# The inverse of the gated delta rule: at two of its three levels, X is copied from a transpose of its own transpose, in place of a third product

## The reference

```python
kk = jnp.einsum('bhnid,bhnjd->bhnij', k, k)
m = jnp.where(strict, beta[..., :, None] * kk * decay, 0.0)
rhs = jnp.concatenate([v * beta[..., None], k * (beta * jnp.exp(g))[..., None]], axis=-1)
sol = lax.linalg.triangular_solve(m, rhs, left_side=True, lower=True, unit_diagonal=True)
...
v_new = u_c - jnp.einsum('bhcd,bhde->bhce', w_c, state)
```

## Time and profile before

| what | value |
|---|---|
| median of 3 runs | 1093.03 us (1093.01 to 1093.15) |
| profiled execution, its own time | 1092.93 us |
| span of that execution, first to last instruction | 1091.6 us |
| granted TensorE clock, mean | 0.999 |
| PE busy | 1079.7 us (99%) |
| DVE busy | 542.6 us (50%) |
| ACT busy | 562.0 us (51%) |
| POOL busy | 436.7 us (40%) |
| L643, PE and PEld records | 64 and 64, 8 of each per head and level |
| L2028 and L2037 | 8 instructions each |

### The profile page before, as it was taken

One profiled execution on the slowest core, in us unless ns is written; L12 is line 12 of the kernel. 1 busy time (PEld: TensorE's weight loads), 2 busy tenths in 40 slices (PEclk: granted clock), 3 DMA queues, 4 the chain that ended last, 5 costly groups with the idle time before them and its releaser, 6 DMA issues.

```text
span 1091.6 us, 14798 instructions
## 1 busy us (share of the span) xinstructions
PE 1079.7 (99%) x5661; PEld 885.1 (81%) x5661; DVE 542.6 (50%) x1135; ACT 562.0 (51%) x1042; POOL 436.7 (40%) x236
## 2 busy tenths in 40 slices
PE   8999999999999999999999999999999999999998
PEld 7877878788888888898778787789888888888886
DVE  3739789698765224152445455535111115544444
ACT  6546767767777642353556566554222224333333
POOL 4334342352532444552242332345444446444441
PEclk9999999999999999999999999999999999999999
DMA  9133121221312232722222321232333334332212
GB/s 258 50 96 88 48 70 48 68 68 47 86 53 78 78 97 97 245 70 75 79 77 69 87 78 59 78 94 79 99 97 97 97 97 134 98 98 97 97 56 77
DMA packets 140528, 97.23 MB, mean 89 GB/s; under 512 B 9013, under 2 KB 125090, under 8 KB 140458
## 3 DMA queue, kind: packets, MB, share of 16 engines
q1 hardware_dynamic: 138728, 95.03, 29.7%
q10 hardware_dynamic: 1730, 1.25, 0.4%
HBM read 94.14 MB, written 2.91 MB: 89 GB/s over the span
## 4 chain that ended last, share of the span: by engine, by line
PE 85%; DVE 10%; issue 2%; ACT 2%; DMA 1%; SPq 0%; POOL 0%; DVEq 0%; ACTq 0%
PE bank L481 24%; PE bank L1194 14%; PE bank L1212 14%; PE bank L522 5%; PE bank L891 4%; PE bank L865 4%; PE bank L875 4%; PE bank L1225 2%; DVE s L2089 1%; DVE g L1896 1%; DVE bank L2011 1%; DVE multipliers L2009 1%; PE bank L496 1%; PE bank L1040 1%; PE bank L1002 1%
## 5 line engine op out<-in xcount | busy, mean ns | idle before, releaser
L2472 POOL TENSOR_TENSOR ring<-raw_ring,ring 128x1024 fp32r<-128x1024 f32 x160 | 389.4, 2437 | 566.8 <-ACT ring L1239 566.8
L481 PE MATMUL bank<-hT,ring 128*128 128x512 f32 x1536 | 392.0, 402 | 0.5 <-ACT rawsb L1314 0.5
L481 PEld LDWEIGHTS bank<-hT,ring 128*128 128x128 f32 x1536 | 278.5, 188 | 58.7 <-issue 6.5
L1239 ACT CAST ring<-raw_ring 128x1024 fp32r<-128x1024 f32 x160 | 167.3, 1047 | 109.5 <-PE bank L1212 88.8
L1194 PE MATMUL bank<-hT,ring 128*128 128x512 f32 x672 | 152.5, 389 | 0.0
L1212 PE MATMUL bank<-ring,ring_u 128*128 128x512 f32 x672 | 152.5, 389 | 0.0
L1212 PEld LDWEIGHTS bank<-ring,ring_u 128*128 128x128 f32 x672 | 126.1, 188 | 26.2
L1194 PEld LDWEIGHTS bank<-hT,ring 128*128 128x128 f32 x672 | 126.1, 188 | 26.1
L2447 DVE TENSOR_TENSOR ring_u<-u,ring_u 128x1024 fp32r<-128x1024 f32 x32 | 80.7, 2529 | 73.8 <-ACT ring_u L1811 73.8
L2452 DVE TENSOR_TENSOR u<-u 128x512 f32<-128x512 f32 x32 | 22.9, 715 | 138.8 <-ACT u L1818 138.8
L1818 ACT ACTIVATE u<-bank 128x512 f32<-128x512 f32 x32 | 19.1, 598 | 114.8 <-PE bank L1194 108.3
(11 more groups left out here) (293 smaller groups left out, 1474.4 us busy)
## 6 DMA issues: line engine op xcount, KB each, us to landing
raw_ring<-in_w_in SPq DMA_DIRECT2D x144, 256.0 KB, 3.3
raw_ring<-in_w_up SPq DMA_DIRECT2D x64, 256.0 KB, 3.2
raw_ring<-in_w_down SPq DMA_DIRECT2D x64, 256.0 KB, 2.8
raw_ring<-in_w_out SPq DMA_DIRECT2D x32, 256.0 KB, 2.9
x<-in_x SPq DMA_DIRECT2D x8, 512.0 KB, 5.0
raw_ring<-in_w_branch_sb SPq DMA_DIRECT2D x8, 256.0 KB, 2.8
raw_ring<-in_w_branch_gdn SPq DMA_DIRECT2D x8, 256.0 KB, 3.3
cum<-cums SPq DMA_DIRECT2D x4, 512.0 KB, 5.1
```

Of the source, the lines that this page charges most:

```text
L481: p = pe.matmul(bank, m.slab_k8(n % 4)[:, a, k, :], m.hT[:, b, k, :], start=term == 0, stop=term == 23)
L1239: act.copy(m.ring[:, q, 0, :], m.raw_ring[:, q, :]).then_inc(s.slab_hi[q], 1)
L2472: pool.tensor_tensor(m.ring[:, q, 1, :], m.raw_ring[:, q, :], m.ring[:, q, 0, :].bitcast(F32), ALU.subtract).then_inc(s.slab_lo[q], 1)
```

## The change

`delta_level_second` keeps only the product into bank 6, and Y is stored without gaps, so that ScalarE's copy is contiguous and no zeros are needed: `delta_zero` and its signal go. A new function `delta_level_T` has TensorE transpose the four chunks of XT, once its half has been updated, into bank 7, and signals `lev_T`. A new function `delta_level_X` on VectorE copies the half of it that X lacks to X. The counts of the signals `inv` and `lev_ps` stay as they were. The order on TensorE and VectorE is changed with it.

```diff
--- before.py
+++ after.py
@@ -295,7 +295,7 @@
 
         self.diag, self.steps = one("diag"), one("steps")
 
-        self.inv, self.lev_c, self.lev_ps, self.lev_y, self.lev_zero = one("inv"), one("lev_c"), one("lev_ps"), one("lev_y"), one("lev_zero")
+        self.inv, self.lev_c, self.lev_ps, self.lev_y, self.lev_T = one("inv"), one("lev_c"), one("lev_ps"), one("lev_y"), one("lev_T")
 
         self.state_ps, self.state, self.w_set = one("state_ps"), one("state"), one("w_set")
         self.o_sum, self.o_dve, self.o_act, self.ogd_lo = one("o_sum"), one("o_dve"), one("o_act"), one("ogd_lo")
@@ -629,19 +629,19 @@
         Y, w = CX[l % 2], 1 << l
         pe.wait_ge(s.lev_y, 3 * i + l - 3)
         pe.wait_ge(s.inv, 7 * i + 2 * (l - 3))
-        if l < LEVELS[-1]:
-            pe.wait_ge(s.lev_zero, 2 * i + l - 3)
         if l == LEVELS[0]:
             pe.wait_ge(s.k_gate, 3 * i + 3)
             pe.wait_ge(s.gram_set, 2 * i + 2)
         for c in range(4):
             o = banks[6][:, c * 64:(c + 1) * 64].rearrange("p (b w) -> p b w", w=w)
-            p = pe.matmul(o, chunk(X, c), by_level(chunk(Y, c), l)[:, :, 1, :], start=True, stop=True)
-        if l < LEVELS[-1]:
-            for c in range(4):
-                o = banks[7][:, c * 64:(c + 1) * 64].rearrange("p (b w) -> p b w", w=w)
-                p = pe.matmul(o, chunk(Y, c), by_level(chunk(X, c), l)[:, :, 0, :], start=True, stop=True)
+            p = pe.matmul(o, chunk(X, c), Y[:, c * 64:(c + 1) * 64].rearrange("p (b w) -> p b w", w=w), start=True, stop=True)
         p.then_inc(s.lev_ps, 1)
+
+    def delta_level_T(i, l):
+        pe.wait_ge(s.inv, 7 * i + 2 * (l - 3) + 1)
+        for c in range(4):
+            p = pe.transpose(chunk(banks[7], c), chunk(XT, c), ident)
+        p.then_inc(s.lev_T, 1)
 
     def delta_solve(i):
         pe.wait_ge(s.inv, 7 * (i + 1))
@@ -748,6 +748,8 @@
         delta_level_first(i, 4)
         tiles.to(98)
         delta_level_second(i, 4)
+        tiles.to(103)
+        delta_level_T(i, 4)
         tiles.to(108)
         delta_level_first(i, 5)
         tiles.to(109)
@@ -758,7 +760,7 @@
         stick_z(i, 2)
         tiles.to(121)
         delta_level_first(i, 6)
-        tiles.to(127)
+        delta_level_T(i, 5)
         tiles.to(135)
         delta_level_second(i, 6)
         tiles.to(144)
@@ -809,15 +811,18 @@
     delta_level_first(i, 4)
     tiles.to(146)
     delta_level_second(i, 4)
+    tiles.to(150)
+    delta_level_T(i, 4)
     tiles.to(153)
     delta_level_first(i, 5)
-    tiles.to(155)
-    delta_level_second(i, 5)
     tiles.to(156)
     stick_av(i, 0)
     stick_z(i, 1)
-    tiles.to(159)
+    tiles.to(158)
+    delta_level_second(i, 5)
+    tiles.to(163)
     delta_level_first(i, 6)
+    delta_level_T(i, 5)
     tiles.to(172)
     delta_level_second(i, 6)
     tiles.to(177)
@@ -1396,9 +1401,8 @@
         act.activation(Ca, Ca, ACT.Exp).then_inc(s.decay_exp, 1)
 
     def delta_level(i, l):
-        w = 1 << l
         act.wait_ge(s.lev_ps, 6 * i + 2 * (l - 3) - 1)
-        act.copy(by_level(CX[l % 2], l)[:, :, 1, :], banks[5][:, 0:T // 2].rearrange("p (cb w) -> p cb w", w=w)).then_inc(s.lev_y, 1)
+        act.copy(CX[l % 2][:, 0:T // 2], banks[5][:, 0:T // 2]).then_inc(s.lev_y, 1)
 
     def delta_w(i):
         act.wait_ge(s.state_ps, 9 * i + 2)
@@ -2024,17 +2028,15 @@
         dve.wait_ge(s.diag, 7 * i + 7)
         dve.tensor_tensor(whole(X), in_blocks(m.diag_inv), block32, ALU.mult).then_inc(s.inv, 1)
 
-    def delta_zero(i, l):
-        dve.memset(by_level(CX[l % 2], l)[:, :, 0, :], 0.0).then_inc(s.lev_zero, 1)
-
     def delta_level(i, l):
         w = 1 << l
         dve.wait_ge(s.lev_ps, 6 * i + 2 * (l - 3))
         half = by_level(XT, l)[:, :, 1, :]
         dve.tensor_tensor(half, half, banks[6][:, 0:T // 2].rearrange("p (cb w) -> p cb w", w=w), ALU.subtract).then_inc(s.inv, 1)
-        if l < LEVELS[-1]:
-            half = by_level(X, l)[:, :, 0, :]
-            dve.tensor_tensor(half, half, banks[7][:, 0:T // 2].rearrange("p (cb w) -> p cb w", w=w), ALU.subtract).then_inc(s.inv, 1)
+
+    def delta_level_X(i, l):
+        dve.wait_ge(s.lev_T, 2 * i + l - 3)
+        dve.tensor_copy(by_level(X, l)[:, :, 0, :], by_level(banks[7], l)[:, :, 0, :]).then_inc(s.inv, 1)
 
     def delta_u(i):
         dve.wait_ge(s.state_ps, 9 * i + 1)
@@ -2114,19 +2116,19 @@
         stick_soft(i, 0)
         delta_values(i)
         delta_gram(i)
-        delta_zero(i, 4)
         delta_substitute(i, 0, 15)
         delta_blocks(i)
         least(gate, m.rawg, s.g_sig, 4 * i + 3, s.g_dve)
         stick_soft(i, 1)
         delta_level(i, 4)
         times(qg, qT, misc, s.decay_exp, 3 * i + 1, s.qg)
-        delta_zero(i, 5)
+        delta_level_X(i, 4)
         times(gate, m.rawg, gate, s.g_sig, 4 * i + 4, s.g_dve)
         stick_gate(i)
         delta_conv(i + 1, 0, qT)
         delta_level(i, 5)
         delta_conv(i + 1, 1, kT)
+        delta_level_X(i, 5)
         stick_soft(i, 2)
         delta_level(i, 6)
         least(MT, qT, s.q_sig, 4 * i + 7, s.q_dve)
```

## The result

The changed kernel takes 1097.01 us (median of 10 runs, 1095.07 to 1097.92) against 1093.12 us before (10 runs): ratio 1.0029, 95% interval 1.0021 to 1.0038. It is 3.9 us slower.

What follows compares the result with a forecast made beforehand. It took VectorE, held by GpSimd, to bound heads 0 to 2: three times 0.19 us won (0.57), head 3 unchanged, so 1092.93 became 1092.36, plus 0.10 for the median: 1092.5 us. Own range 1092.0 to 1093.1, 60 in 100.

Steps and rivals of the forecast that it cites:

- What bounds the kernel: Heads 0 to 2: VectorE is the chain up to the solve; TensorE has 0.66 us of slack there despite 99% busy.
- TensorE's terms: Per level, transposes at 0.44 us replace a third product of 0.89; a new level 4 wait of about 0.9 us.
- VectorE's 0.19 us a head: Heads 0 to 2: removing level 4's zeros starts the chain 0.19 us sooner per head, together 0.57 us.
- The lower bound: Heads 0 to 2: 0 us won per head, if the handover covers the zeros' place.
- the zeros of level 5: Heads 0 to 2: removing these 0.20 us of VectorE work wins nothing, since its products wait for GpSimd.
- Head 3, the step that failed: Head 3: no change in time, bounds 1.3 us won to 0.7 lost; the solve within 0.3 us of its old place.
- GpSimd overtakes the last scan: Rival, heads 0 to 2: GpSimd's split precedes the second scan, some 2.5 us lost per head, 1100 us; 6 in 100.
- TensorE as the bound: Rival: TensorE's busy share decides, so 8 x 0.45 = 3.6 us won, 1089.4 us; 10 in 100.
- VectorE not held by GpSimd: Rival: no hold at the level 5 zeros' place, so 3 x 0.39 us won, 1091.9 us; 12 in 100.
- Transposes at 0.27 us each: Rival: four cost 1.09 us against the third product's 0.89; 1.8 us lost, 1094.8 us; 5 in 100.
- The threshold of 0.25 us a transpose: The price per transpose from which the costly-transposes rival was said to decide.
- Head 3 somewhat worse: Rival: the copy blocks merge_least and a tile matmul waits for its bank; 0.5 to 1 us, 1093.3 us; 7 in 100.

Runs made afterwards that it cites:

- e7: The e5 kernel with heads 0 to 2's level 4 transposes moved directly behind the first product of level 5: 1092.22 us, 0.9990 of the kernel before.
- e8: The e7 kernel with VectorE's gate product in heads 0 to 2 moved from ahead of level 5 to near the head's end: 1090.67 us.
- e9: The kernel before the change, with only VectorE's gate product of heads 0 to 2 moved to the head's end: 1091.85 us, 0.9985 of the kernel before.
- e1: The changed kernel with ScalarE's slab split in head 3's merge tile 6 moved behind that tile's Abs, Exp and Ln: 1092.96 us, 0.9998 of the kernel before.
- e4: The changed kernel with thirteen more merge-stream tile matmuls ahead of head 3's solve instead of behind it: 1094.91 us, 1.0013 of the kernel before.
- e5: The changed kernel with head 3's level 5 transposes ahead of the first product of level 6 instead of behind it: 1092.14 us, 0.9990 of the kernel before.
- e3: The change in head 3 alone, heads 0 to 2 as in the kernel before: 1097.44 us, 1.0033 of the kernel before.

## Why the prediction was wrong

**What bounds the kernel.** Right for heads 0 to 2: VectorE, held by GpSimd, sets the solve's start. e7 shows it from TensorE's side (the 3.2 us before the transposes removed, 1.3 net, no change) and e8 and e9 from VectorE's (one product less in the chain, 1.5 and 1.6 us).

**TensorE's terms.** The transposes' 0.44 us per four were 0.39 and 0.45, the third product's 0.89 is gone, the new wait was 1.07 in place of 0.9. In heads 0 to 2 none of it moved the time, as said: TensorE was at the solve at 117.58 - 0.67 = 116.91, where the working had 116.9.

**VectorE's 0.19 us a head.** The direction was right, the size half: 0.10. The zeros stood behind a copy (L1997 at 86.92) for which the substitution had to wait in any case; from that copy to the first product it was 0.53 us before (87.45) and is 0.40 after, and that product is longer by 0.06 (0.28 in place of 0.22). The lower bound named this: the handover covers part of the zeros' place. That the zeros of level 5 are worth nothing was right.

**Head 3, the step that failed.** "I take no change. Bounds: 1.3 us won to 0.7 lost." It was 4.9 us lost. That figure is for the profiled execution, and the solve came 2.05 us later on the clock of the trace, where it was to stay within 0.3. The step followed VectorE's queue and had TensorE's part nearly exact (the first product of level 6 at 326.63, I had 326.65). The scans came 0.55 us later, I had 0.3: the copy to X began at 328.33, where the working let it begin at 327.98 with the end of the transposes. It left out two things, and both were put at nothing without a reason. First, it didn't set GpSimd's row beside the scans, though heads 0 to 2 had been argued from exactly such rows: the split had a lead of 331.64 - (329.65 + 0.86) = 1.1 us to lose, the later scans took 0.55 of it, and the earlier split 1.06; the blocked scan then cost 2.1 us (3.94 in place of 1.80). Second, it priced waiting at its length only, and the clock behind the wait cost 2.7 us more. The rival "GpSimd overtakes the last scan" was the right mechanism, with 6 in 100 and in the wrong head: in heads 0 to 2 the lead shrank about as said (to 115.27 less about 114.80, 0.47 us) and held. That the size came out was luck: the working had ScalarE's split follow VectorE's convolution, but in the trace ScalarE waited there for TensorE's attention product (1.71 us for L700, up to 108.12; before up to 108.58), which came 0.46 us sooner. It is the same path by which the split came sooner in head 3. The runs show both halves: e1 takes the overtaking away and brings 4.0 us back, e4 leaves it and takes the clock's part away.

**The other rivals.** TensorE as the bound: false, by e7 and by the 0.10 us that heads 0 to 2 won. VectorE not held by GpSimd: false, by the three gaps of 0.55 after and by e8. Transposes at 0.27 us each: false, 0.10 to 0.11; the Trainium skill ("TensorE: Matmul & The Clock Gate", "Part 4: PE-mode transpose") names bf16 beside its 275 ns, these transposes are f32. The threshold of 0.25 us a transpose doesn't come out of the prediction's own figures: eight transposes use up the 0.5 us between 116.9 and 117.40 from 0.17 each on. Head 3 somewhat worse: this was real, and small. In the changed kernel the tile matmul behind the transposes stands still for 0.44 us, and goes on 0.12 behind the end of merge_least (328.67 + 0.68 = 329.35), which fits that rival's reason:

```profile
329.47 0.76 PEld L481 LDWEIGHTS bank<-hT,ring 128*128 128x128 f32 x4 [0.44 <-issue]
```

e1 has this and the wait of 1.01 us, and its time says that together they cost no more than the lighter inverse gave; e5 doesn't have the 0.44 and is 0.8 us faster than e1.

The lock of the Trainium skill ("SBUF — State Buffer", "SBUF: two separate sides"), exclusive and held for the whole instruction, agrees with these traces: in head 3 GpSimd has the split up to 330.58 + 2.74 = 333.32, and the second scan ends 0.82 us later, at 334.14, when a scan takes 0.86. Its consequence that the order of arrival decides is what the prediction should have carried into head 3. For the clock, the Trainium skill ("TensorE: Matmul & The Clock Gate", "Why this matters for your kernels") warns of idle gaps of TensorE in the middle of a kernel; here a wait of 3.15 us lowered the granted clock to 0.50, in the changed kernel and in e3, and one of 1.01 us (e1) did not.

## What to carry to other kernels

Where VectorE and GpSimd both work on SBUF, write down for each long GpSimd instruction its lead over the VectorE instruction next to it, and recompute it for every move on any engine: a shift of half a microsecond can cost the whole instruction. Work saved on TensorE counts as such a move, since it lets ScalarE, and GpSimd behind it, start sooner. A wait that a change adds can cost far more than its length where TensorE's granted clock falls (here 2.7 us by the clock beside 3.15 us of wait, in e3 1.5 us beside the same wait); TensorE work kept back for that place took the clock's part away (e4). And less work on the busiest engine gives nothing in a stage where another engine makes the chain: find that first.

## What was not expected of the hardware

With a wait of 3.15 us the granted clock of TensorE fell to 0.50, from 334.6 to 341.4 us, which cost 2.7 us, nearly as much as the wait itself; e3, with the same wait, had it from 336.4 to 339.8 us and lost 1.5 us by it. The time of this case varies with it: the changed kernel's ten runs lie between 1095.07 and 1097.92, the kernel before's within 1.2 us. Its three runs at 1095.1 to 1095.5 have a mean granted clock of 0.997 to 0.998, its seven at 1096.96 and above one of 0.996 to 0.997, as if the low clock lasted shorter in the three. e3 shows that its length does vary between executions, but no profile of one of the three was taken, so their cause stays open. A zeroing of 128x256 that shows as 0.27 us held VectorE's chain for about 0.1, since the next instruction had a wait of its own.
